# Memory attention after the indexer, and some of the top-k rounds beside it

## The reference, cut to what matters

```
y_a = hgrn2_mixer(hq, hf, hi, hg, ...)            # recurrence
y_b = pool_mixer(pz, ...)                         # trailing means
y_c = dsa_mixer(sq, sk, sv, iq, ik, iw)           # sparse attention with an indexer
mkv = rms_norm(mem, norm_mem) @ w_mem_kv          # 256 memory tokens
y_m = mem_attention(mq, mk, mv)                   # dense attention into them
merged = sum over the branches of sigmoid(u @ w_gate[b]) * (y @ w_branch[b])
```

```
score = sum over 8 heads of w[t,h] * relu(q_idx[t,h] . k_idx[s])
top_val, top_idx = lax.top_k(score, 256)
```

## Time and profile before

| what | value |
|---|---|
| median of three executions | 3433.82 us |
| the profiled execution | 3438.68 us |
| its span, first to last instruction | 3436.6 us |
| TensorE busy in the span | 3082.6 us (90%) |
| VectorE busy in the span | 1361.6 us (40%) |
| ScalarE, GpSimd busy | 934.0 us (27%), 965.2 us (28%) |
| granted TensorE clock, mean | 0.952 of full speed |

### The profile page before, as it was taken

The page is one execution under the profiler, slowest core; times in us unless marked ns, Lnnn a source line. Parts: engine busy times, 40 slices in busy tenths (PEclk is TensorE's granted clock), DMA queues, the critical chain, the costliest instruction groups (busy, mean ns, idle before and its releaser), DMA issues. The chain is left out here.

```text
span 3436.6 us, 37947 instructions
## 1 busy us (share of the span) xinstructions
PE 3082.6 (90%) x14355; PEld 2441.9 (71%) x14355; DVE 1361.6 (40%) x2015; ACT 934.0 (27%) x1465; POOL 965.2 (28%) x738
## 2 busy tenths in 40 slices
PE   5999999999899994998898999878893999999996
PEld 2888778777666873787676777656682888888884
DVE  3244520110011026454338999842127233323335
ACT  3355522222222233222425222143222111111112
POOL 1433222223312321211121333301424333323322
PEclk9999999999999997999999999989996999999997
DMA  4211021111212111111110111102110111111111
GB/s 174 57 35 35 10 95 49 43 34 46 70 30 77 52 43 55 41 31 31 38 33 22 42 43 46 43 1 72 49 43 11 51 43 49 49 49 49 43 49 49
DMA packets 250638, 161.58 MB, mean 47 GB/s; under 512 B 23156, under 2 KB 240812, under 8 KB 249389
## 3 DMA queue, kind: packets, MB, share of 16 engines
q1 hardware_dynamic: 248674, 154.85, 15.2%
q10 hardware_dynamic: 1867, 5.41, 0.4%
HBM read 151.78 MB, written 8.45 MB: 47 GB/s over the span
## 5 line engine op out<-in xcount | busy, mean ns | idle before, releaser
L298 PE MATMUL ps<-h_hi,w_hi 128*128 128x512 f32 x2880 | 1149.2, 399 | 166.4 <-DMA masks<-k_levels 34.8
L298 PE MATMUL ps<-h_lo,w_hi 128*128 128x512 f32 x2880 | 1133.9, 394 | 0.0
L298 PE MATMUL ps<-h_hi,w_lo 128*128 128x512 f32 x2880 | 1132.8, 393 | 0.0
L278 POOL TENSOR_TENSOR w_lo<-raw,w_hi 128x512 fp32r<-128x512 f32 (+2 forms) x524 | 609.4, 1185 | 1579.4 <-ACT w_hi L271 1579.4
L298 PEld LDWEIGHTS ps<-h_hi,w_hi 128*128 128x128 f32 x2880 | 548.8, 191 | 301.4 <-issue 144.4
L298 PEld LDWEIGHTS ps<-h_hi,w_lo 128*128 128x128 f32 x2880 | 548.0, 190 | 117.1
L298 PEld LDWEIGHTS ps<-h_lo,w_hi 128*128 128x128 f32 x2880 | 548.6, 190 | 113.1 <-issue 1.7
L271 ACT ACTIVATE w_hi<-raw 128x512 fp32r<-128x512 f32 (+2 forms) x524 | 268.5, 563 | 392.7 <-PE ps L298 207.5
L2864 DVE TENSOR_TENSOR acc<-acc,ps 128x1024 f32<-128x1024 f32 x176 | 215.1, 1222 | 31.3 <-PE ps L2893 31.2
L2855 DVE TENSOR_TENSOR act<-gate,ps 128x1024 f32<-128x1024 f32 x22 | 26.9, 1221 | 456.3 <-PE ps L298 456.3
L1109 DVE TENSOR_TENSOR part<-sig,ps 128x1024 f32<-128x1024 f32 x40 | 48.6, 1216 | 373.7 <-PE ps L298 373.7
(11 more groups left out here) (385 smaller groups left out, 3642.9 us busy)
## 6 DMA issues: line engine op xcount, KB each, us to landing
raw<-in_w_in SPq DMA_DIRECT2D x88, 512.0 KB, 4.0
raw<-in_w_ffn_gate_up SPq DMA_DIRECT2D x44, 512.0 KB, 3.7
raw<-in_w_gate SPq DMA_DIRECT2D x32, 512.0 KB, 3.8
raw<-in_w_ffn_down SPq DMA_DIRECT2D x22, 512.0 KB, 3.5
w_ada<-in_w_ada SPq DMA_DIRECT2D x8, 1024.0 KB, 5.2
raw<-in_w_out SPq DMA_DIRECT2D x16, 512.0 KB, 3.7
x_tok<-in_x ACTq DMA_DIRECT2D x1, 4096.0 KB, 20.6
residual_gate<-in_w_ada SPq DMA_DIRECT2D x8, 512.0 KB
```

The lines of the kernel that those rows point to most:

```text
L278: pool.tensor_tensor(w_lo[:, s, cut], raw[:, s, cut], w_hi[:, s, cut].bitcast(F32), ALU.subtract).then_inc(split.sem, 1)
L298: last = pe.matmul(dst, w[:, chunk[0] % 2, k], x(k), start=(k == 0 and n == 0), stop=(k == kt - 1 and n == 2))
```

## The change

The stage order becomes `hgrn`, `indexer`, `memory_attention`, first `merge`. Eight of the 64 half rounds move into `memory_attention` on VectorE: four at its start, ahead of the normalisation of the memory tokens, and four between `mem_lo` and the evictions of keys and values. In the merge the numbers of half rounds by unit and place go from ((1, 2), (1, 2), (1, 1)) twice, which is 16 in an iteration, to ((1, 1), (1, 2), (1, 1)) twice, which is 14. As `score` has to live through the memory attention, two of its buffers now share the place of others: `prob` is a view of `mem_tok`, `prob_t` a view of `mem32`.

```
-        def memory_attention(y_hi_t, y_lo_t, following):
+        def memory_attention(y_hi_t, y_lo_t, following, beside):
...
-                prob = sb(sc, "prob", [P, 2, H, NMEM])
-                prob_t = sb(sc, "prob_t", [P, 2, 2 * H, P])
+                prob = mem_tok[:].rearrange("p b (h k) -> p b h k", k=NMEM)
+                prob_t = mem32[:].rearrange("p (b j) (u c) -> p b (j u) c", b=2, c=P)
...
                 @block.vector
                 def _(dve):
+                    beside(dve, 0, 0, 0)
                     dve.wait_ge(sq_ready.sem, sq_ready.at(2))
...
                     dve.tensor_tensor(mem_lo[:], mem32[:], mem_hi[:].bitcast(F32), ALU.subtract)...
+                    beside(dve, 0, 0, 1)
                     for m in range(4):
                         dve.wait_ge(used.sem, after(used, 2 + m, 0, 6))
...
-                hgrn(ya_hi, ya_lo, memory_source)
-                ym_hi, ym_lo = pair("m")
-                memory_attention(ym_hi, ym_lo, indexer_source)
-                yb_hi, yb_lo = pair("b")
+                hgrn(ya_hi, ya_lo, indexer_source)
+                yb_hi, yb_lo = pair("b")
+                ym_hi, ym_lo = pair("m")
...
-                indexer(yb_hi, yb_lo, score, kv_t, merge_source(from_abm))
+                best = sb(second, "best", [P, len(SCORED), 8])
+                indexer(yb_hi, yb_lo, score, kv_t, memory_source)
+                memory_attention(ym_hi, ym_lo, merge_source(from_abm), top_rounds(score, best, ((4, 4),), 0))
+                top_steps.close()
                 acc = sb(second, "acc", [P, KT, T])
-                best = sb(second, "best", [P, len(SCORED), 8])
-                merge(acc, from_abm, False, sparse_source, beside=top_rounds(score, best, ((1, 2), (1, 2), (1, 1)) * 2))
+                merge(acc, from_abm, False, sparse_source, beside=top_rounds(score, best, ((1, 1), (1, 2), (1, 1)) * 2, 1))
```

More of the change, by code:

```diff
@@ L2113, in _ @@
                     for t in range(2):
-                        act.activation(prob[:, t].rearrange("p h k -> p (h k)"), mem_tok[:, t], ACT.Square,
+                        act.activation(mem32[:, t * 4:t * 4 + 4].rearrange("p h k -> p (h k)"), mem_tok[:, t], ACT.Square,
                                        accum_out=sums[:, t:t + 1]).then_inc(sq_ready.sem, 1)
@@ L2496, in indexer, with top_rounds @@
             chunk_passed(8)
-        def top_rounds(score, best, halves_of):
+        def top_rounds(score, best, halves_of, first_step):
             per = (len(SCORED) + 1) * sum(n for unit in halves_of for n in unit)
@@ L2509, in beside @@
                 if u == 0 and place == 0:
-                    top_steps.open(i, per)
+                    top_steps.open(i, per if first_step else 0)
                 for _ in range(halves_of[u][place]):
```

## The result

The changed kernel takes 3441.99 us in the median of 9 runs (3439.78 to 3446.38), the kernel before 3433.82 (3433.05 to 3439.59), also 9 runs. The ratio is 1.0022, with a 95% interval of 1.0012 to 1.0033: slower by 8.2 us, where +5.1 was forecast. The median lies within the predicted range, 0.5 us from its upper end, but 1.1 us above the 3440.9 at which the likeliest case alone ended. The interval excludes 1, so there is a loss; at a margin of 2% it would still be called the same time. A second measurement of the same kernel gave 1.0023 (experiment 10). Executions of one kernel fall at two levels (before: 3433.1 to 3434.7 or 3439.2 to 3439.6; after: 3439.8 to 3443.0 or 3445.9 to 3446.4), and both profiled executions are of the upper one.

What follows compares the result with a forecast made beforehand. TensorE and the splitting of its weights pace the merge, VectorE only its tail. Merge -3.2, first four 0, second four +8.3, stage order 0 make +5.1 us on 3433.8: 3438.9 us, range 3434.5 to 3442.5.

Steps and rivals of the forecast that it cites:

- likeliest case: Whole kernel: +5.1 us to 3438.9 us, own range 3434.7 to 3440.9, chance 0.80.
- slow rival: Memory attention: low clock lasts over the first three or four attention blocks, +9.4 us in all, 3443.2 us; chance 0.15.
- The merge's pace: First merge: TensorE and the splitting of its weights set the step of 14.3 us, with or without top-k.
- fast rival: First merge: VectorE sets the pace; in full 3401.3 us, by small waits 3430.7; chance 0.05 (0.03 and 0.02).
- The merge's tail: End of first merge: VectorE's lag behind TensorE's last matmul shrinks from 11.5 to about 8.3 us, -3.2 us.
- order of stages: Moving the stage costs 0, within 1 us: indexer and memory attention start slow, merge fast, two slow starts as before.
- The first four half rounds: Start of memory attention: 20.4 us of VectorE work covered by TensorE's query products with 0.6 us to spare, cost 0.
- The prediction's own sign: Memory attention: `mem_tok` turns follow the query products without idle; an idle there would show the prediction wrong.
- the fallback in the text: Start of memory attention: if the cover fell short by 1 us, the cost would be 1 us, not the group.
- The second four: Memory attention after `mem_lo`: copies and attention start 7.6 us later, +8.3 us with low clock, range 6.9 to 9.1.
- Its bound in the stage: Memory attention: a loss of 10.1 us or more there would decide for the slow rival.

Runs made afterwards that it cites:

- experiment 10: The changed kernel measured once more without an edit: 3441.51 us, ratio 1.0023 to the kernel before.
- experiment 8: The kernel before with all 64 half rounds left out of the merge, so no top-k: 3427.99 us, ratio 0.9979.
- experiment 4: The kernel before with eight half rounds left out, 56 in the merge, order of stages as before: 3430.95 us, ratio 0.9992.
- experiment 3: The changed kernel without its first group of four half rounds, 60 of 64 done: 3437.68 us, ratio 1.0009 to the kernel before.
- experiment 5: The changed kernel with GpSimd splitting the third weight chunk ahead of its power in the memory attention: 3438.14 us, ratio 1.0009 to the kernel before.
- Experiment 2: The changed kernel without its second group of four half rounds, 60 of 64 done: 3430.79 us, ratio 0.9994 to the kernel before.
- experiment 1: The changed kernel with only the new stage order, all 64 half rounds in the merge: 3434.92 us, ratio 1.0007 to the kernel before.
- experiment 9: The changed kernel with half rounds four at start, two behind mem_lo, two before the merge's loop, rest early, third splitting first: 3429.14 us, ratio 0.9987.
- experiment 7: The changed kernel with the merge's 56 half rounds placed early, none behind the last product: 3438.04 us, ratio 1.0009 to the kernel before.
- experiment 6: The kernel before with all 64 half rounds placed early in the merge, order of stages as before: 3427.87 us, ratio 0.9979.

## Why the prediction was right, and where it was not

**The range.** The measured 3442.0 lies outside the likeliest case's own range (to 3440.9). It is inside the stated one because that was widened to 3442.5 for half of the slow rival, whose mechanism did not come. That part is luck.

**The merge's pace (right).** Taking out 8 half rounds left the step at 14.3 us, and taking out all 64 did too (experiment 8). VectorE's 96% said nothing of who sets the pace. (The prediction set it against the 75% of the weight loads; TensorE's matmuls were busy for 337.3 of 361.9 us, 93%, so it was not far ahead.) By the Trainium skill, page "Perfetto Trace Analysis", section "Identifying the Most-Contended Engine", VectorE would have been the bottleneck; 319 us less of its work made the merge 7.5 us shorter, so the measurement decides against that rule here. The fast rival falls in both its forms: TensorE's 13.0 us of waits for `w_lo` are the same without any half rounds.

**The merge's tail (right).** -3.2 us forecast, -3.2 measured in the changed kernel, -3.4 in experiment 4. The whole merge of the changed kernel is 3.2 us shorter only because it began at low clock, as before; where it began at full clock, in experiments 3 and 5, it is 4.9 to 5.0 us shorter (see the order of stages below).

**The first four half rounds (the step that failed).** The prediction held that the two query products cover the whole group with 0.6 us to spare, and that GpSimd's late splitting of the third chunk is covered too. It asked only who needs that splitting, not beside whom it would then run. The late power releases VectorE's normalisation and GpSimd's splitting at the same moment, and the two TENSOR_SCALAR take 1.77 us each instead of 0.75. That eats the 0.6 us, and TensorE idles for 1.00. Experiment 2 gives this to the first group, experiment 5 removes it by order alone. The price is 1.4 us up to the key and value products (1.3 against experiment 1), where 0 was taken, and as the order of stages shows below, it goes with a slow start of the merge that costs 1.6 more. The prediction's own sign, an idle ahead of the turns of `mem_tok`, says that this part was wrong; the fallback in the text ("if the cover fell short by 1 us, the cost would be 1 us") had the size but not the cause. The Trainium skill, page "SBUF — State Buffer", section "Who interferes with whom", says that VectorE in its two-port mode, for which it lists tensor_scalar, and GpSimd share a pair of ports under an exclusive lock, and that the one who comes second stalls. The trace agrees as far as it goes: 0.75 us became 1.77, and the four instructions took 3.54 us together (1793.17 to 1796.71), not far from the 3.97 that they take one after another (2.55 and 1.42). That it is this lock was not tested apart from the overlap itself.

**The second four (mechanism right, size near).** Forecast: evictions and turn of `v_t` 7.6 us late, 8.3 with the clock. Measured: 7.4 us of delay and 0.3 us behind it, 7.7. Against experiment 1, which has the same order of stages, the group alone (experiment 3) costs 9.7 us, over the prediction's upper end of 9.1. The gap between 7.7 and 9.7 is in the attention: it takes 34.5 us in experiments 1 and 2, and 36.9 to 37.4 in all other runs, experiment 9 and the kernel before among them, where TensorE had idled for only 0.52 us ahead of `v_t`. So the long idle costs 0.3 us there or 2.9, by which of the two it is compared with, and what decides between them stays open.

**The order of stages (right in sum when it stands alone, wrong in the changed kernel).** Ratio 1.0007 for it alone. The prediction had the indexer slow, the memory attention slow as before and the merge fast, so that nothing was lost. The slow start of the indexer came (+0.8). The merge's first 3.4 us ran at full clock in experiment 1 but not in the changed kernel:

```profile
1853.60:1857.00 3.40, 3.37 (x15) 2.81 (x16) 3.40 (x5) 1.68 (x3) 0.89 (x2) 1.00 0.54 159
```

```profile
1864.30:1867.70 3.40, 3.40 (x9) 2.66 (x10) 3.40 (x5) 1.63 (x3) 0.87 (x2) 0.54 0.52 154
```

The columns are those of the earlier trace rows, first experiment 1, then the changed kernel: 9 matmuls in place of 15, at a granted clock of 0.54. The end of the stage ahead of it and its last idle (1.53 us) are the same. The runs fall into two groups by one thing. In the changed kernel, its repetition and experiments 2 and 7, where the tokens are late and TensorE idles for 0.95 to 1.03 us ahead of their turn, the granted clock in the merge's first 3.4 us is 0.53 to 0.56, and TensorE needs 17.2 us from its first matmul to the second unit. In experiments 1, 3, 5 and 9, without that idle, it is 1.00 and 15.6 us. Experiment 5 turns the slow start into the fast one by nothing but the order of GpSimd's splitting and its power. So the merge's fast start was lost through the lateness of the tokens. How an idle of 1 us some 67 us earlier does that, no run shows.

**The slow rival** (low clock over several blocks, +9.4) did not come: it adds 3.5 us to the 1.5 that the likeliest case already counted for the low clock, and the attention from the turn of `v_t` on grew by 0.3 us against before. Its bound in the stage, a loss of 10.1 us, was not reached (9.1). The clock was low for a short while, as the columns of the earlier trace rows show for the two stretches of 7 us from the turn of `v_t` on (after the change):

```profile
1827.00:1834.00 7.00, 4.43 (x22) 3.26 (x24) 3.02 (x6) 4.21 (x13) 0.00 (x0) 0.74 0.00 0
1834.00:1841.00 7.00, 6.95 (x50) 5.28 (x50) 5.68 (x9) 4.43 (x17) 0.00 (x0) 0.77 0.01 2
```

**The sum.** By the profiles: 0.5 + 0.8 + 9.1 - 3.2 - 0.1 = 7.1 of the 7.2 us, where 5.1 was forecast. The 2 us between are 0.5 ahead of the change, 0.8 for the indexer's slow start, 0.8 in the memory attention (1.4 for the late tokens, less 0.2 for a shorter delay of `v_t` and 0.4 for less low clock than forecast), and -0.1 behind it. The medians put 8.2 between the kernels in the first measurement and 7.6 in the second. Of what lies between 7.2 and these no stage's row gives an account; the interval of the first, some 4 to 11 us, takes in both.

## What to carry to other kernels

Before work is taken off a busy engine, look at whether anyone waits for it inside the loop; if only the stage's tail shows it, a different placing of the same work (64 half rounds early instead of spread, experiment 6) gains twice what moving an eighth of it away did (6.3 us against 3.2), and costs nothing elsewhere. When a step is delayed into idle time, ask not only who needs it but what starts at the same moment on the other engines: cover of 0.6 us was lost to two instructions that did not run beside GpSimd before. And an end of a stage has a floor made of the chain behind the last matmul (here product and addition, 3.9 us), to be added up before a tail is promised away.

## What the runs showed of the hardware

A TENSOR_SCALAR of 128x1024 float32 took 0.75 us alone and 1.77 beside GpSimd's splitting of 128x512, which itself took 2.98 us for two instead of 2.55 (the first 1.29 as alone, the second 1.73). MAX8 and MATCH_REPLACE8 lose nothing beside GpSimd: at each of their six widths the mean with a GpSimd instruction running at the same time is within 3 ns of the mean without one (kernel before; at 128x1024, 1209 ns for MATCH_REPLACE8 in both, 11 and 21 times).

A stage far ahead of the change, with the same code in all kernels, is not equally long in all profiles: from TensorE's first matmul in it at about 777 us to that of the next stage it lasts 298.2 to 298.4 us in the profiles of before, after and experiment 1, and 294.6 to 295.0 in the nine others. The granted clock differs inside it, here in the kernel before and in experiment 4:

```profile
927.00:977.00 50.00, 50.00 (x198) 36.80 (x198) 7.69 (x12) 12.43 (x17) 8.94 (x6) 0.95 0.09 25
```

```profile
927.00:977.00 50.00, 50.00 (x212) 37.47 (x211) 8.53 (x13) 12.44 (x17) 10.86 (x7) 0.99 0.07 21
```

TensorE is busy for all of the 50 us in both, with 198 matmuls at 0.95 and 212 at 0.99. In the kernel before, the clock fell within this time, behind 10 us at 1.00 in which TensorE had no idle:

```profile
940.00:950.00 10.00, 10.00 (x45) 7.34 (x44) 2.30 (x4) 1.59 (x3) 2.99 (x2) 1.00 0.18 52
950.00:956.00 6.00, 6.00 (x18) 2.91 (x18) 0.00 (x0) 0.00 (x0) 0.00 (x0) 0.74 0.00 0
```

So profiles of two kernels may differ by 3.5 us in a stage that nobody touched, and stages are better compared one by one than by the sum.
